# Dilated attention on one Trainium2 core: four of a head's eight square weight chunks in seven products instead of three

## The reference, cut to what matters

```python
def dilated_attention(h, w_qkv, q_gain, k_gain, w_o, rel_bias):
    qkv = (h @ w_qkv).reshape(B, S, N_SW_GROUPS, SW_GROUP_COLS)
    ...
    for g, (window, dil) in enumerate(SW_GROUPS):
        q, k, v = jnp.split(qkv[:, :, g], [nqk, 2 * nqk], axis=-1)
        q = rmsnorm(q.reshape(B, S, N_HEADS, HEAD_DIM), q_gain[g])
        k = rmsnorm(k.reshape(B, S, N_HEADS, HEAD_DIM), k_gain[g])
        ...
        p = jnp.exp(logits - m)
        l = jnp.sum(p, axis=-1, keepdims=True)
        o = jnp.einsum('bnrhqk,bnkrhe->bnqrhe', (p / l).astype(v.dtype), vv)
        ...
    o = alpha[0][..., None] * outs[0] + alpha[1][..., None] * outs[1] + alpha[2][..., None] * outs[2]
    return o.astype(h.dtype).reshape(B, S, ATTN_WIDTH) @ w_o
```

## Time and profile before

| | us |
|---|---|
| median of three runs (2515.15 to 2516.18) | 2515.76 |
| the profiled execution | 2516.16 |
| its span, first to last instruction | 2514.4 |
| TensorE matmul busy | 2502.3 |
| TensorE weight loads busy | 2094.3 |
| VectorE busy | 2086.3 |
| ScalarE busy | 1413.1 |
| GpSimd busy | 28.9 |

### The profile page before, as it was taken

The page is one execution under the profiler, slowest core; times in us unless marked ns, Lnnn a source line. Parts: engine busy times, 40 slices in busy tenths (PEclk is TensorE's granted clock), DMA queues, the critical chain, the costliest instruction groups (busy, mean ns, idle before and its releaser), DMA issues.

```text
span 2514.4 us, 30571 instructions
## 1 busy us (share of the span) xinstructions
PE 2502.3 (100%) x11859; PEld 2094.3 (83%) x11859; DVE 2086.3 (83%) x2337; ACT 1413.1 (56%) x1527; POOL 28.9 (1%) x36
## 2 busy tenths in 40 slices
PE   9999999999999999999999999999999999999999
PEld 8888888888888888887888888888888888888887
DVE  6656666999999998988777878776699999999897
ACT  6545555655666655556545545544566565656554
POOL 1000000000000000000000000000000000000000
PEclk9999999999999999999999999999999999999999
DMA  8544554646465556566556666654464655556654
GB/s 281 184 159 158 190 187 145 223 159 228 166 214 183 194 195 218 192 208 193 152 158 186 186 201 186 182 170 151 141 229 167 228 174 179 206 171 228 213 166 160
DMA packets 362228, 472.29 MB, mean 188 GB/s; under 512 B 18997, under 2 KB 215813, under 8 KB 361968
## 3 DMA queue, kind: packets, MB, share of 16 engines
q1 hardware_dynamic: 360448, 465.64, 56.7%
q0 software_dynamic: 1408, 4.76, 0.6%
q10 hardware_dynamic: 240, 0.10, 0.0%
HBM read 468.31 MB, written 3.68 MB: 188 GB/s over the span
## 4 chain that ended last, share of the span: by engine, by line
PE 89%; DVE 5%; ACT 3%; DMA 2%; issue 1%; SPq 0%; ACTq 0%; DVEq 0%
PE psum L1906 38%; PE psum L1910 19%; PE psum L1792 8%; PE psum L1793 8%; PE psum L1799 8%; PE psum L2002 1%; DVE w_lo L1077 1%; DMA w_raw<-in_b_w_qkv 1%; ACT w_hi L631 1%; PE psum L1917 1%; PE psum L1919 1%; PE psum L1918 1%; PE psum L2127 1%; ACT w_hi L642 1%; DMA w_raw<-in_f_w_up 1%
## 5 line engine op out<-in xcount | busy, mean ns | idle before, releaser
L1906 PE MATMUL psum<-w_hi,xT 128*128 128x512 f32 x4056 | 993.6, 391 | 0.9
L1906 PEld LDWEIGHTS psum<-w_hi,xT 128*128 128x128 f32 x4056 | 758.2, 188 | 161.6 <-DVE xT L1449 5.1
L631 ACT ACTIVATE w_hi<-w_raw 128x2048 fp32r<-128x2048 f32 (+1 forms) x338 | 615.3, 1822 | 432.9 <-PE psum L1910 322.7
L1077 DVE TENSOR_TENSOR w_lo<-w_raw,w_hi 128x2048 fp32r<-128x2048 f32 (+1 forms) x338 | 725.6, 2167 | 86.5 <-ACT w_hi L631 86.2
L1910 PE MATMUL psum<-w_lo,xT 128*128 128x512 f32 x2028 | 527.7, 389 | 0.1
L1910 PEld LDWEIGHTS psum<-w_lo,xT 128*128 128x128 f32 x2028 | 380.5, 188 | 79.9 <-DVE w_lo L1077 1.0
L1792 PE MATMUL psum<-w_hi,xT 128*128 128x512 f32 (+1 forms) x1008 | 362.7, 369 | 2.2 <-DVE phase L1574 2.1
L1793 PE MATMUL psum<-w_hi,xT 128*128 128x512 f32 (+1 forms) x1008 | 356.0, 363 | 0.0
L1085 DVE TENSOR_TENSOR w_lo<-w_raw,w_hi 128x2048 fp32r<-128x2048 f32 (+1 forms) x118 | 255.9, 2180 | 56.8 <-ACT w_hi L642 56.5
L642 ACT ACTIVATE w_hi<-w_raw 128x2048 fp32r<-128x2048 f32 (+1 forms) x118 | 215.3, 1830 | 107.0 <-PE psum L1910 59.3
L1069 DVE TENSOR_TENSOR w_lo<-w_raw,w_hi 128x2048 fp32r<-128x2048 f32 (+1 forms) x98 | 188.7, 1941 | 59.4 <-ACT w_hi L620 59.0
(11 more groups left out here) (199 smaller groups left out, 1869.6 us busy)
## 6 DMA issues: line engine op xcount, KB each, us to landing
w_raw<-in_f_w_up SPq DMA_DIRECT2D x352, 512.0 KB, 4.9
w_raw<-in_f_w_down SPq DMA_DIRECT2D x176, 512.0 KB, 4.9
w_raw<-in_b_w_qkv SPq DMA_DIRECT2D x192, 256.0 KB, 3.9
w_raw<-in_a_w_qkv SPq DMA_DIRECT2D x94, 512.0 KB, 4.5
w_raw<-in_b_w_qkv SPq DMA_DIRECT2D x256, 128.0 KB, 2.7
w_raw<-in_a_w_o SPq DMA_DIRECT2D x16, 1024.0 KB, 5.0
w_raw<-in_b_w_qkv SPq DMA_DIRECT2D x32, 512.0 KB, 6.2
w_raw<-in_b_w_o SPq DMA_DIRECT2D x16, 1024.0 KB, 5.7
```

The lines of the kernel that those rows point to most:

```text
L631: nc.scalar.activation(w_hi[:, slot, cols], w_raw[:, slot, cols], ACT.Copy).then_inc(hi_ready, 1)
L1077: nc.vector.tensor_tensor(w_lo[:, slot, cols], w_raw[:, slot, cols], w_hi[:, slot, cols], ALU.subtract).then_inc(lo_ready, 1)
L1906: pe.matmul(o, x[:, h, P * m:P * (m + 1)], hi, start=start and h == 0, stop=False)
```

## The change

Chunk 7 joins the seven-product form, and a head becomes 16 positions. Positions 4 to 15 are now one by one: std 0, std 1, one 4, std 2, sum 4, one 5, sum 5, one 6, sum 6, one 7, sum 7, std 3. `B_STEPS` stays as it is. `mixT` and the mixed x of this layer hold four pairs; the part of SBUF for phases and the scratch of GpSimd's DMAs shrink for it. Four things are rearranged: the next head waits at its start for the combine's first add alone (`b_p6_out`) and for the rest only at position 4; VectorE's `b_take` stands ahead of the sums and the split; in the first `one` of a head the matmuls into `other` come third, behind a wait for ScalarE's copy of the transposed probabilities; the constants' loads wait for weight chunk 2.

```diff
+FOUR = (("std", 0), ("std", 1), ("one", 4), ("std", 2), ("sum", 4), ("one", 5), ("sum", 5), ("one", 6), ("sum", 6), ("one", 7),
+        ("sum", 7), ("std", 3))
+B_MIXED = (4, 5, 6, 7)
...
-B_ENTRIES = tuple(("all", j) for j in range(4)) + THREE
-MIX_PAIRS = len(MIXED)
+B_ENTRIES = tuple(("all", j) for j in range(4)) + FOUR
+MIX_PAIRS = len(B_MIXED)
...
-            pool.wait_ge(x_in[3], 16)
+            pool.wait_ge(w_in[2], landed(A0 + 2))
...
-                chain.step(nc.vector.tensor_tensor(u[:, 1, :], p6, u[:, 0, :], ALU.add))
-                chain.settle()
+                nc.vector.tensor_tensor(u[:, 1, :], p6, u[:, 0, :], ALU.add).then_inc(b_p6_out, 1)
+                dve.wait_ge(b_p6_out, h + 1)
...
+                    if e == 3:
+                        b_take(c + e, h, odd)
                     if e + LEAD + 1 == B_ONES[0]:
                         b_add_weights(c + B_ONES[0], c + B_SUMS[0])
                     split_ahead(c, e)
                     for one, to in zip(B_ONES[1:], B_SUMS[1:]):
                         if e + LEAD + 3 == one:
                             b_add_weights(c + one, c + to)
-                    if e == 3:
-                        b_take(c + e, h, odd)
...
                 high_made()
-                high(x[0], 0, c, 1, psum[:, other, :], start)
                 high(x[1], 0, c, 2, psum[:, own, :])
                 high(mix[3], 0, c, 3, psum[:, own + 2, :])
+                if first_free is not None:
+                    first_free()
+                high(x[0], 0, c, 1, psum[:, other, :], start)
...
+                    def first_free():
+                        at_least(pe, b_pT_act, h)
...
                     if e == 0:
+                        at_least(pe, b_p6_out, h)
+                    if e == 4:
                         at_least(pe, b_combined, h)
...
-                    if e == B_ONES[0] and not is_turn(h, 0):
-                        pe.wait_ge(b_pT_act, h)
...
-    nc = bacc.Bacc("TRN2", target_bir_lowering=False, num_devices=1, dynamic_dma_scratch_size=4096)
+    nc = bacc.Bacc("TRN2", target_bir_lowering=False, num_devices=1, dynamic_dma_scratch_size=2048)
```

More of the change, by code:

```diff
@@ L84, with mixed @@
 DOWN_ENTRIES = [(what, p, j) for p, form in enumerate(((6, 5), (3, 6))) for what, j in down_pass(*form)]
-B_ENTRIES = tuple(("all", j) for j in range(4)) + THREE
-MIX_PAIRS = len(MIXED)
+B_ENTRIES = tuple(("all", j) for j in range(4)) + FOUR
+MIX_PAIRS = len(B_MIXED)
+def mixed(n):
+    return B_MIXED if n == 2 else MIXED
 B_ONES = [e for e, (what, j) in enumerate(B_ENTRIES) if what == "one"]
@@ L271, in trunk @@
         psum = ctx.enter_context(nc.psum_tensor("psum", [P, 8, 512], F32))
-        phase = sb("phase", [P, 14848])
+        phase = sb("phase", [P, 14720])
         def part(at, *dims):
             n = int(np.prod(dims))
-            assert at + n <= 14848
+            assert at + n <= 14720
             v = phase[:, at:at + n]
@@ L306, in trunk @@
         b_sq = part(7296, G * M, 256)
[L307 to L310, removed]
+        b_bias = part(8832, G, SEQ)
+        b_mask = part(9600, G, SEQ)
+        b_row = part(10368, SEQ)
+        b_oT = part(10624, KB, SEQ)
         hT = part(0, FB, SEQ)
@@ L314, in trunk @@
         x_f32 = part(11264, 2 * MIX_PAIRS, SEQ)
-        mix_f32 = part(12800, 4, MIX_PAIRS, P)
+        up_mix, b_mix = part(12800, 4, len(MIXED), P), part(6144, 4, len(B_MIXED), P)
         c_gate = part(13312, 4, SEQ)
@@ L382, in trunk @@
         down_quarter = sem("down_quarter")
-        b_p1_out, b_combined, b_summed = sem("b_p1_out"), sem("b_combined"), sem("b_summed")
+        b_p1_out, b_p6_out, b_combined, b_summed = sem("b_p1_out"), sem("b_p6_out"), sem("b_combined"), sem("b_summed")
         h_mixed, h_mix_hi, h_mix_lo = sem("h_mixed"), sem("h_mix_hi"), sem("h_mix_lo")
@@ L668, in take_xT @@
                     at = 256 * (k % 2)
-                    if n > 0 and k // 2 in MIXED:
-                        nc.scalar.activation(x_f32[:, 2 * MIXED.index(k // 2) + k % 2, :],
+                    if n > 0 and k // 2 in mixed(n):
+                        nc.scalar.activation(x_f32[:, 2 * mixed(n).index(k // 2) + k % 2, :],
                                              psum[:, xT_bank(n, k), at:at + 256], ACT.Copy,
@@ L834, in mix_high @@
                 act.wait_ge(mix_ready, n)
-                pairs = slice(0, len(MIXED))
-                nc.scalar.activation(mixT[:, :, pairs, 0, :], mix_f32[:, :, pairs, :], ACT.Copy).then_inc(mix_hi, 1)
+                nc.scalar.activation(mixT[:, :, 0:len(mixed(n)), 0, :], b_mix if n == 2 else up_mix, ACT.Copy).then_inc(mix_hi, 1)
             def conv_init(layer, odd, tile, t, tg):
@@ L1110, in mix_x @@
             def mix_x(n):
-                dve.wait_ge(xT_hi, KB * n + 2 * MIXED[-1] + 2)
-                pairs = slice(0, len(MIXED))
-                x = x_f32[:, 0:2 * len(MIXED), :].rearrange("p (i k) c -> p i k c", k=2)
+                dve.wait_ge(xT_hi, KB * n + 2 * mixed(n)[-1] + 2)
+                x = x_f32[:, 0:2 * len(mixed(n)), :].rearrange("p (i k) c -> p i k c", k=2)
                 a11, a12, a21, a22 = (x[:, :, k, P * m:P * (m + 1)] for m in range(M) for k in range(2))
-                s1, s2, s3, s4 = (mix_f32[:, i, pairs, :] for i in range(4))
+                s1, s2, s3, s4 = ((b_mix if n == 2 else up_mix)[:, i, :, :] for i in range(4))
                 nc.vector.tensor_tensor(s3, a11, a21, ALU.subtract)
@@ L1125, in mix_low @@
                 dve.wait_ge(mix_hi, n)
-                pairs = slice(0, len(MIXED))
-                nc.vector.tensor_tensor(mixT[:, :, pairs, 1, :], mix_f32[:, :, pairs, :], mixT[:, :, pairs, 0, :],
+                pairs = slice(0, len(mixed(n)))
+                nc.vector.tensor_tensor(mixT[:, :, pairs, 1, :], b_mix if n == 2 else up_mix, mixT[:, :, pairs, 0, :],
                                         ALU.subtract).then_inc(mix_lo, 1)
@@ L1951, in last_square, with fast_one @@
                         ins.then_inc(last_part, 1)
-            def fast_one(c, x, mix, own, other, start, stop, high_made, low_made):
+            def fast_one(c, x, mix, own, other, start, stop, high_made, low_made, first_free=None):
                 high_made()
-                high(x[0], 0, c, 1, psum[:, other, :], start)
                 high(x[1], 0, c, 2, psum[:, own, :])
                 high(mix[3], 0, c, 3, psum[:, own + 2, :])
+                if first_free is not None:
+                    first_free()
+                high(x[0], 0, c, 1, psum[:, other, :], start)
                 low_made()
@@ L2147, in b_entry_of @@
                 elif what == "std":
-                    plain_square(c, x, own, False, 2 * j + 2 == KB, high_made, low_made)
+                    plain_square(c, x, own, False, j == 3, high_made, low_made)
                 else:
-                    i = MIXED.index(j)
+                    def first_free():
+                        at_least(pe, b_pT_act, h)
+                    i = B_MIXED.index(j)
                     mix = [mixT[:, s, i, :, :] for s in range(4)]
-                    (fast_one if what == "one" else fast_sum)(c, x, mix, own, other, i == 0, i == len(MIXED) - 1,
-                                                              high_made, low_made)
+                    begun, ended = i == 0, i == len(B_MIXED) - 1
+                    if what == "one":
+                        fast_one(c, x, mix, own, other, begun, ended, high_made, low_made, first_free if begun else None)
+                    else:
+                        fast_sum(c, x, mix, own, other, begun, ended, high_made, low_made)
             def upper_first(c, x, own, h):
```

## The result

The changed kernel takes **2572.5 us** (median of five runs, 2571.2 to 2577.2) against 2515.2 before (five runs): 2.3% slower, ratio 1.0227 with a 95% interval of 1.0214 to 1.0240. Slower was forecast, with a mechanism and a size of 31 us; the size is 57. The profiled execution took 2571.8 us with a span of 2570.0, 55.6 us above's kernel.

The account below looks back on a forecast made before the run. TensorE was taken to bound the kernel in every stage. 2516.2 us of the profiled execution + 41.3 of waits - 10.4 of gains = 2547.1, so 2547 us; forecast itself 2541 to 2552, range 2536 to 2560.

Parts of the forecast that it names:

- (a): One more fast pair in each of eight heads: 24 matmuls of 0.226 us fewer, 5.4 us less.
- (b): Start of a head: TensorE's wait shrinks from all four adds of the combine to the first; 3.0 us less.
- (c): Position 3: VectorE's copy of the first products moves ahead of split and sums; 1.1 us less, in the first head.
- (d): Opening: the constants' transfers start after weight chunk 2, 1.5 us earlier, so TensorE's 0.9 us wait goes.
- The softmax 2.9 us late: Previous head's attention on VectorE: copy, first sum and narrow split now precede the softmax, which starts 2.9 us late.
- ScalarE's 1.5 us: Position 6: the pair's two high matmuls wait for ScalarE's copy, about 1.5 us of the 5.9 us a head.
- VectorE's copies, 5.9 us in each of seven heads: Position 6, heads 1 to 7: value products wait for VectorE's copies of the transposed probabilities; 7 x 5.9 = 41.3 us more.
- low parts late in the row of pairs: Run of pairs: VectorE never more than a step behind with its low parts; nothing taken, at most 2 us a head.
- the first rival: The clock falls from 2.4 to 1.2 GHz in the new waits of seven heads: +17 us, 2564; chance 0.15.

Follow-up runs that it names:

- experiment 4: The kernel before, with the rearrangements of the change but without the fourth pair: 2511.5 us, ratio 0.9983.
- Experiment 5: The changed kernel with ScalarE's copy of the first bank and VectorE's combine ahead of the next head's split in position 14: 2558.6 us, ratio 1.0173.
- the second run of 7: Repeat of the changed kernel with positions 6 and 7 swapped, VectorE's copy behind the split in heads 1 to 7, combine ahead of the split: 2506.9 us.
- experiment 1: The changed kernel with the value products of the previous head's attention after position 7 instead of position 6: 2531.8 us, ratio 1.0064.
- experiment 6: The changed kernel with two neighbours swapped, the plain square in position 6 and the pair's first half in position 7: 2526.8 us, ratio 1.0043.
- experiment 3: The changed kernel with VectorE's copy of the first products behind the weight sum and split again in heads 1 to 7: 2545.2 us, ratio 1.0120.
- experiment 2: The changed kernel with unused 128-column matmuls before the value products in heads 1 to 7: 2584.1 us with 36, 2558.8 us with 18.

## Why the prediction was right and wrong

**(a) 24 matmuls, 5.4 us: right.** 24 fewer in the busy line, 4.1 us between the two versions where little else waits (medians of 11 and 5 runs whose ranges don't meet).

**(b) The start of a head, 3.0 us gained: wrong in sign in the changed kernel.** "The wait at the start of a head shrinks from all four adds of the combine to the first of them" is true, and without the fourth pair it went as forecast (experiment 4). I took the combine's time as the only thing in the way and didn't ask when VectorE comes to it. It stands behind a split whose weights land late; the first add itself came late, and 6.6 us were lost where 3.0 were to be gained. Experiment 5 shows that it is the place in the queue; why the weights land late stays open.

**(c) and (d), 1.1 and 0.9 us: right** in the changed kernel's profile (1.0 and 0.9). (d) is open in its worst case, since three other profiles have a wait for the constants' copies (1.8 us in experiment 4, 1.0 in 5, 1.6 in the second run of 7).

**The softmax 2.9 us late, ScalarE's 1.5 us, VectorE's copies, 5.9 us in each of seven heads: right.** Measured: 4.9 us between copy and softmax, as worked out; waits of 1.25 and 4.42 us, 39.7 in all for 41.3. Experiments 1 and 6 give the handover its cover back and remove the 4.42 us in two different ways, and experiment 3 takes off the part that came from the softmax, by the amount that the chain gives. "I take nothing for this", of low parts late in the row of pairs, held as well: no such wait in any run, even with the pairs in a row.

**The step that failed is the first rival's.** I priced the fall of the clock at nothing in the sum, gave it 0.15, and left the full fall in every head out of the range; its upper end, 2560, is five of seven falls by my price. It happened in seven of seven. This alone carries the time out of the range (2547 + 16.6 = 2563.7); the miss of (b) alone would not have (2556.7). The argument against it, "no row of the kernel before shows a fall", was none: that kernel has no wait over 1.1 us inside a dilated head, so it could not show one. The Trainium skill, "TensorE: Matmul & The Clock Gate", section "HAM oscillation — how this bites in real kernels", says that a gap can throttle the engine and that every return is paid for; the trace agrees, with seven falls of the granted clock. My price for all seven, 17 us, was right within a microsecond: 16.6 by the balance, 13.7 to 16.2 between the changed kernel and the filled wait. That is in part luck: it took for every head that the lower clock lasts as long as the wait and falls on matmuls alone, but the value products lost between 1.5 and 2.9 us, and in experiment 5, with the same waits, the seven cost 11.9. With the clock and (b)'s sign the same sum comes to 2547.1 + 16.6 + 9.6 - 1.6 for the slightly shorter waits = 2571.7, where the profiled execution took 2571.8.

## What to carry to other kernels

When a position in a hand-written order becomes shorter, list which handovers of other work used it as cover, and move them with the cover; the operation count says nothing of this. On a TensorE-bound kernel, price each new wait twice: its length, and half of the matmul time that follows at 1.2 GHz, unless rows with waits as long show that the clock stays. And an early release helps only if the instruction that gives it stands early enough in its own engine's queue.

## What the runs showed of the hardware that was not expected

Waits much shorter than the 4.4 us of the changed kernel can lower the clock. In experiment 6, waits at the starts of eight heads, 1.6 to 2.7 us by the distances of starts, were followed by a fall in five. Length alone doesn't decide: the longest of them, 2.7 us, and one of 2.4 had no fall, while two of 1.9 had one. Single waits of 1.8 us were followed by one in experiments 2 and 4; seven of 1.7 us in experiment 1 were not, nor was the 1.1 us of the kernel before. Experiment 3's kernel, with seven waits of 2.7 us, has a mean granted clock from 1.000 to 0.994 in four runs of the same program, and its times spread over 14 us where those of the others spread over 6.3 at most. What decides was not tried.

A float32 matmul of 128 columns that is not a transpose stands in the trace as two and takes 0.22 us (36 records in 4.2 us in experiment 2), the transposes of the same size 0.11.
